# Order of the four matmuls of a contraction tile: long, long, short, short becomes long, short, long, short

## The reference, cut to what matters

```python
def hybrid_layer(x, mem, ...):
    h = rmsnorm(x, g_mix)
    proj = h @ w_in                                   # 2048 -> 12296 columns
    fq, fk, fv, ff, lx, lg, mq, gate_logits = jnp.split(proj, cuts, axis=-1)
    ... y_fox = forgetting_attention(q, k, v, log_f)  # 8 heads x 128
    ... y_lru = rg_lru(conv(lx)) * gelu(lg)           # 1024 channels
    mk, mv = jnp.split(rmsnorm(mem, g_mem) @ w_mem_kv, 2, axis=-1)
    ... y_mem = memory_attention(qm, km, vm)          # 4 heads x 256
    y_d = jnp.einsum('bsnc,ncd->bsnd', branches, w_branch)
    merged = jnp.sum(sigmoid(gate_logits + b_gate) * y_d, axis=2)
    x = x + merged @ w_out
    up = causal_depthwise_conv(rmsnorm(x, g_ffn) @ w_ffn_up, ...)
    u_act, u_val = jnp.split(up, 2, axis=-1)
    return x + (gelu(u_act) * u_val) @ w_ffn_down
```

## Time and profile before

| | |
|---|---|
| median of 3 runs | 1699.79 us (1699.44 to 1701.18) |
| profiled execution, its own time | 1701.18 us |
| span of its trace | 1699.3 us |
| mean granted TensorE clock | 0.99 |
| TensorE matmul busy | 1665.1 us (98%) |
| TensorE weight load busy | 1439.1 us (85%) |
| VectorE / ScalarE / GpSimd busy | 67% / 52% / 7% |
| HBM read | 303.64 MB, 180 GB/s over the span |

### The profile page before, as it was taken

How to read it: one execution, slowest core, us unless ns; L and a number is a source line. 1 busy time by engine, 2 the same in 40 slices (tenths; PEclk the granted TensorE clock), 3 DMA queues, 4 the chain that set the end, 5 groups by cost and what they waited for, 6 DMA issues and landing times.

```text
span 1699.3 us, 27268 instructions
## 1 busy us (share of the span) xinstructions
PE 1665.1 (98%) x9386; PEld 1439.1 (85%) x9386; DVE 1136.0 (67%) x1302; ACT 888.8 (52%) x1135; POOL 126.5 (7%) x90
## 2 busy tenths in 40 slices
PE   4999999999999999999999999999999999999998
PEld 3878888888888888888888888888888888888887
DVE  8786767668765657466576677777777777544443
ACT  3466667555655544545455555555555555433432
POOL 7132212120000000000001000000000000000000
PEclk7899999999999999999999999999999999999999
DMA  6555556664555666657655665556655566665553
GB/s 211 162 161 161 147 161 200 162 173 136 154 156 186 187 196 184 188 181 192 193 187 187 183 187 180 185 189 197 191 190 178 189 190 196 195 200 195 198 194 109
DMA packets 308044, 306.34 MB, mean 180 GB/s; under 512 B 11744, under 2 KB 307168, under 8 KB 308000
## 3 DMA queue, kind: packets, MB, share of 16 engines
q1 hardware_dynamic: 307056, 302.89, 58.6%
q0 software_dynamic: 944, 2.88, 0.6%
HBM read 303.64 MB, written 2.10 MB: 180 GB/s over the span
## 4 chain that ended last, share of the span: by engine, by line
PE 95%; DVE 3%; DMA 1%; ACT 0%; POOL 0%; issue 0%; SPq 0%; ACTq 0%; DVEq 0%; POOLq 0%
PE psG L339 92%; PE psM L339 3%; DVE XM L1048 1%; DVE W L880 1%; DVE X L1048 0%; DMA mem_raw<-memT 0%; DMA lru_rg<-w_rg 0%; DVE rstd L1101 0%; POOL x_n L1335 0%; PE psM L430 0%; PE psM L428 0%; ACT X L705 0%; ACT L700 0%; ACT W L575 0%; POOL lru_rg L1368 0%
## 5 line engine op out<-in xcount | busy, mean ns | idle before, releaser
L339 PE MATMUL psG<-X,W 128*128 128x512 f32 (+1 forms) x5632 | 992.9, 338 | 0.0
L339 PEld LDWEIGHTS psG<-X,W 128*128 128x128 f32 x5632 | 860.1, 188 | 129.2 <-issue 3.4
L880 DVE TENSOR_TENSOR W<-raw,W 128x1024 fp32r<-128x1024 f32 x568 | 699.6, 1245 | 330.2 <-ACT W L575 327.4
L575 ACT ACTIVATE W<-raw 128x1024 fp32r<-128x1024 f32 x568 | 592.7, 1054 | 351.6 <-PE psG L339 347.0
L339 PE MATMUL psG<-hidden,W 128*128 128x512 f32 (+1 forms) x1408 | 245.4, 337 | 0.0
L339 PEld LDWEIGHTS psG<-hidden,W 128*128 128x128 f32 x1408 | 214.0, 188 | 31.3
L583 ACT ACTIVATE low<-psG 128x512 f32<-128x512 f32 x140 | 83.8, 598 | 238.2 <-PE psG L339 238.2
L339 PE MATMUL psG<-Y,W 128*128 x768 | 134.4, 337 | 0.0
L339 PEld LDWEIGHTS psG<-Y,W 128*128 128x128 f32 x768 | 117.0, 188 | 17.1
L1241 DVE SCALAR_TENSOR_TENSOR up_c<-up_pad,par_sb,up_c 128x256 f32<-128x256 f32 x176 | 77.5, 482 | 42.3 <-ACT up_c L824 36.3
L339 PE MATMUL psG<-merged,W 128*128 128x512 f32 (+1 forms) x512 | 89.3, 337 | 0.0
(11 more groups left out here) (181 smaller groups left out, 790.0 us busy)
## 6 DMA issues: line engine op xcount, KB each, us to landing
raw<-w_in SPq DMA_DIRECT2D x192, 512.0 KB, 4.1
raw<-w_up SPq DMA_DIRECT2D x176, 512.0 KB, 4.6
raw<-w_down SPq DMA_DIRECT2D x88, 512.0 KB, 3.4
raw<-w_branch SPq DMA_DIRECT2D x48, 512.0 KB, 3.3
raw<-w_mem_kv SPq DMA_DIRECT2D x32, 512.0 KB, 3.8
raw<-w_out SPq DMA_DIRECT2D x32, 512.0 KB, 3.5
mem_raw<-memT SPq DMA_DIRECT2D x4, 512.0 KB, 9.0
xs<-xT SPq DMA_DIRECT2D x4, 512.0 KB, 8.6
```

The lines of the kernel that those rows point to most:

```text
L339: return nc.tensor.matmul(*a, skip_group_check=True, **kw)
L575: nc.scalar.activation(W[:, s, :, 0], raw[:, s], ACT.Copy).then_inc(hi_done, 1)
L880: V.tensor_tensor(W[:, s, :, 1], raw[:, s], f32(W[:, s, :, 0]), ALU.subtract).then_inc(lo_done, 1)
```

## The change

For each contraction tile the two loops over the halves `t` become one. The order is then long(t=0), short(t=0), long(t=1), short(t=1). The matmuls themselves, their operands, their number, the waits and the semaphore increment on the last short one of the unit are as before, and so is the order of the additions within each PSUM bank. The diff also adds empty lines at the top of the file, which move the line numbers.

```diff
                         x_hl = operand(kt)
-                        halves = [slice(t * P, t * P + P) for t in range(2)]
-                        for t, ts in enumerate(halves):
+                        for t in range(2):
+                            ts = slice(t * P, t * P + P)
                             if rows_major:
                                 mm(psG[:, b + t, :], x_hl[:, 0, ts], W[:, s, k], start=kt == 0, stop=False)
+                                ins = mm(psG[:, b + t, T:], x_hl[:, 1, ts], W[:, s, k, 0], start=False, stop=kt == last)
                             else:
                                 mm(psG[:, b + t, :], W[:, s, k, 0, ts], x_hl, start=kt == 0, stop=False)
-                        for t, ts in enumerate(halves):
-                            if rows_major:
-                                ins = mm(psG[:, b + t, T:], x_hl[:, 1, ts], W[:, s, k, 0], start=False, stop=kt == last)
-                            else:
                                 ins = mm(psG[:, b + t, T:], W[:, s, k, 1, ts], x_hl[:, 0], start=False, stop=kt == last)
                     ins.then_inc(pe_units, 1)
```

## The result

The changed kernel takes 1716.17 us (median of 4 runs, 1709.41 to 1718.3) against 1700.17 us: ratio 1.009, 95% interval 1.0063 to 1.0116, so 0.9% slower. Its runs differ more than those of before: of nine in all, two took 1708.4 and 1709.4 us and seven 1715.1 to 1719.7, while before stays within 1699.4 to 1701.2 in its four, and within 1696.7 to 1701.3 in all its later ones.

A forecast was written before the change was run, and what follows sets the result against it. TensorE's matmul spacing, 174.2 ns each, was taken to bound the kernel; the new order's terms summed to 2272 steps x 0 = 0 us, leaving the median of 1699.8 us, range 1691 to 1709.

The forecast's parts named there:

- (a): Projection matmuls: each short one newly stands between two long ones, loads alternating likewise; loads stay hidden, price 0.
- the bound of 2.9 ns per step: Four projection matmuls of a contraction tile: at most 2.9 ns less, from the `logits` row; 2272 times, -6.6 us.
- the hook: `logits` matmuls, long and short alternating into one bank: 32 in 5.55 us, 693.8 ns for four, taken as showing no cost.
- TensorE alone sets the time: Whole kernel: weights come early, so a change in the spacing of TensorE's matmuls goes into the time one to one.
- The waits, the signals and the start are unchanged: All engines get the same signals after the same work; TensorE's waits stay 29 us; first 48 us change by 0.
- (b): Projections: two matmuls in a row go into one PSUM bank; price 0, at most +13.2 us.
- The rival that held most of the 0.23 for slower: Second matmul into a PSUM bank waits for the first: 1706.4 us at half the bound, 1713.0 at it; 0.23 with size.
- The rival of the change of size: Every neighbouring matmul has another size: 1 ns at each of two more changes, +4.5 us, 1704.3; 0.23 with the bank.
- The excess grows with the columns: Projection spacings: long some 20 ns above their columns, short 5 to 13, like a stream slightly under one column a cycle.
- The faster rival: Alternation lets a load be drawn ahead across a long matmul: 2.9 ns less per four matmuls, 1693.2 us; chance 0.22.
- an excess of 130 us: Projections: 14 ns per matmul beyond streaming, cause in no row; prediction wrong if it depends on order at full width.

The follow-up runs named there:

- 8 and 8: Against the kernel before: each unit of 4 contraction tiles does all 8 long matmuls, then its 8 short ones; 1702.17 us, ratio 1.0023.
- the reset and the turned tile: Changed kernel, every second group opening with 8 long, then 8 short matmuls, then one tile long, long, short, short; 1694.6 us, ratio 0.9975.
- third profile: The changed kernel run a third time with no edit; 1703.37 us.
- with the reset: Changed kernel, first unit of every second group doing 8 long, then 8 short matmuls, no tile turned after it; 1714.32 us (1712.65 to 1715.22), ratio 1.0096.
- long, short, short, long: Changed kernel with one contraction tile of every second unit in this order; 1718.57 us.
- the kernel with other banks: Changed kernel's alternation, but each long matmul goes to the bank the short one before did not use; 1715.18 us, ratio 1.0105.

## Why the prediction was wrong, point by point

The forecast was no change, 1699.8 us, range 1691 to 1709; measured 1716.17. The step that failed is (a), the price of 0 for a short matmul between two long ones, and with it the bound of 2.9 ns per step that was taken from the hook. No rival had the mechanism of the slowdown with its true price.

- *TensorE alone sets the time, and a change in its spacing goes through one to one.* Right: the spans differ by 5.7 us and the chain's TensorE rows make it up.
- *The waits, the signals and the start are unchanged.* Right to 0.8 us.
- *(b) The same bank costs nothing.* Right, and now shown at full width: ratio 1.0 with 12 of 16 neighbours in one bank. The rival that held most of the 0.23 for slower was false.
- *(a) Each short matmul between two long ones costs 0.* This is the step that failed. The alternation almost alone, with 2 of 16 neighbours in one bank, gave 1.0105. Its term was not 0 but one of two: 173.3 - 174.2 = -0.9 ns per matmul, -8 us over 9088, or 176.7 - 174.2 = +2.5 ns, +23 us.
- *The rival of the change of size* had the place right (more changes of size) and the size wrong: 1 ns at each of two more changes per step, +4.5 us. The slow pattern adds 10 ns per step. And it isn't a price per change: in 16 matmuls, 8 and 8 has two changes and 20 ns above the fast pattern, the order of before eight changes and 13 ns, the fast pattern sixteen and none. The 0.12 after a long and 0.11 after a short one in the earlier trace rows were rounding: to the nanosecond, before has 115 or 116 for the first and 112 to 117 for the second.
- *The excess grows with the columns and looks like a stream a little under one column a cycle; the sum of columns is not changed.* Wrong. Settled, a long matmul has 13 ns above its columns as a short one has; the 20 ns of the long ones in the earlier trace rows were a pattern's. The Trainium skill (TensorE: Matmul & The Clock Gate, Back-to-back issue gap) gives a warm matmul on its own a fixed addition whatever its columns, and says that in a stream of loads and matmuls both set the spacing, which the prediction left out. The form with a fixed addition agrees with the settled runs; its 2.5 ns does not, measured are 13. From spacings at one order I read a law, where the rows held a pattern that only this order makes.
- *The nearest row was the hook.* It has alternation and bank, and I took it for the new order's price. But its stationary tile has 40 columns, and narrow tiles change the patterns: at 32 the short ones are at 118 ns, not 120, and with 64 in the changed order the long rows don't have the slow pattern. It took 5.56 us in the changed kernel, 5.55 before, and so could not show either speed.
- *The faster rival* gave 1693.2 us by its 2.9 ns per step. The fast pattern takes 3.4 ns per step off, and 1694.6 us was reached, but only in another kernel, with the reset and the turned tile; what I held against it, that a load isn't drawn further ahead, is still so in every row.

The last sentence of the prediction named the weak point, an excess of 130 us without a cause in any row, and still the range was made as though its order dependence were bounded by the hook. The bounds should have come from the excess: even a twentieth of it is 6.5 us.

Shown is: the order of sizes sets the spacing; the alternating order has two speeds; one tile in another order can turn one into the other; the bank, the stage, the clock and the waits don't. Argued only: that the seven runs near 1717 us have the slow pattern in the last stages too. 13.9 us more on the third profile's 1703.37 would be 1717.3, and the kernels whose profiles are slow in both long rows took 1712.65 us (with the reset) and 1718.57 (long, short, short, long), which fits. Against it stands that the hook between the two rows changed the speed in all four profiles of an alternating order without a disturbance, so that slow in both was not seen in one. Fast and then slow, as in the kernel with other banks, would be only 4.7 us above slow and then fast. No profile holds such a run, and so the greater part of the 16 us is not shown in a trace of the changed kernel itself. Open: what inside TensorE makes the 13 ns and the patterns, and what at the entry picks one. The width of the stationary tile takes part in it; proportion to the width is excluded.

## What to carry to other kernels

In an unbroken stream of matmuls with a load each, the spacing is a repeating pattern, and reordering equal work can move it by 1 to 2% without a wait, a clock or a byte changing: divide the chain's long rows by their counts, stage by stage, before and after. Where runs of one kernel spread much wider than those of its predecessor (here 11 us against 4.6), look for stages that have two speeds, and judge no order by one profile. A run of one size is a reset, after which, until a hook comes between, what followed was the same every time; with it the better of two patterns can be chosen and not hoped for.

## What was not expected of the hardware

- The same matmuls, with the granted clock at 1.00 (the 2.4 GHz level) in both stretches, hold 173.3 or 176.7 ns per matmul for 700 us on end.
- The fp32r matmuls settle at 13 ns above their columns, for 512 and 256 columns alike, with loads of 128 columns; with stationary tiles of 64 columns short ones are 7 above, with 32 some 11 above.
- A single contraction tile in the order long, long, short, short reverses the speed in groups of 64 matmuls, 11.30 and 11.10 us in turn, and leaves it slow in groups of 176.
- Consecutive matmuls into one PSUM bank at full width, short onto what long has just written, cost nothing that 724.54 us of them show.
